# Attention rounds on TensorE in the order scores, values, turns in place of scores, turns, values

## The reference

```python
s = jnp.einsum('bqhd,bkhd->bhqk', q, k) * scale + bias
p = jax.nn.softmax(jnp.where(mask, s, NEG_INF), axis=-1)
o = jnp.einsum('bhqk,bkhd->bqhd', p, v)
```

## Time and profile before

| | |
|---|---|
| median of 3 runs | 1201.32 us (1199.18 to 1202.43) |
| profiled execution | 1197.51 us, span 1195.4 us |
| busy: TensorE, VectorE, ScalarE, GpSimd | 1030.1, 665.0, 476.1, 167.4 us |
| mean granted clock of TensorE | 0.922 of full speed |
| turns L475 | 240 records, median 273 ns |
| values L487 | 160 records, median 275 ns |
| copies L548 | 80, median 471 ns |

### The profile page before, as it was taken

The page is one execution under the profiler, slowest core; times in us unless marked ns, Lnnn a source line. Parts: engine busy times, 40 slices in busy tenths (PEclk is TensorE's granted clock), DMA queues, the critical chain, the costliest instruction groups (busy, mean ns, idle before and its releaser), DMA issues.

```text
span 1195.4 us, 17516 instructions
## 1 busy us (share of the span) xinstructions
PE 1030.1 (86%) x6902; PEld 933.6 (78%) x6902; DVE 665.0 (56%) x1247; ACT 476.1 (40%) x693; POOL 167.4 (14%) x171
## 2 busy tenths in 40 slices
PE   5698967868899779788779999997998878999995
PEld 2597736657899568776769999996996778999994
DVE  5654176867455666463574545456443575454555
ACT  0243333433344553336533443432446443434340
POOL 1001668700096000000001000000001000000000
PEclk9799876979999989888888999998999898999998
DMA  9863424224345503631055545452452053454540
GB/s 371 326 232 110 182 106 159 89 71 141 110 177 192 189 2 134 227 106 36 1 194 194 192 176 195 173 199 86 169 182 86 1 194 133 167 206 162 207 161 35
DMA packets 22535, 181.53 MB, mean 152 GB/s; under 512 B 3599, under 2 KB 3999, under 8 KB 6743
## 3 DMA queue, kind: packets, MB, share of 16 engines
q1 hardware_dynamic: 18112, 167.88, 38.2%
q0 software_dynamic: 2384, 10.88, 2.8%
q10 hardware_dynamic: 1991, 2.12, 0.6%
HBM read 179.82 MB, written 1.05 MB: 151 GB/s over the span
## 4 chain that ended last, share of the span: by engine, by line
PE 71%; DVE 14%; ACT 6%; DMA 4%; issue 2%; POOL 1%; ACTq 1%; SPq 0%; DVEq 0%; POOLq 0%
PE G L777 12%; PE G L778 12%; PE G L779 12%; PE S L842 7%; PE S L844 7%; PE S L843 7%; PE T L396 3%; DMA early<-in_ada_w 3%; DVE wlo L1307 2%; PE T L475 2%; ACT whi L1066 2%; DVE hTl L413 2%; PE S L924 1%; PE G L489 1%; PE G L487 1%
## 5 line engine op out<-in xcount | busy, mean ns | idle before, releaser
L777 PE MATMUL G<-whi,hTh 128*128 128x256 f32 (+4 forms) x884 | 275.3, 311 | 29.3 <-DVE hTl L413 28.1
L778 PE MATMUL G<-wlo,hTh 128*128 128x256 f32 (+4 forms) x884 | 271.3, 307 | 0.0
L779 PE MATMUL G<-whi,hTl 128*128 128x256 f32 (+4 forms) x884 | 270.7, 306 | 0.0
L1307 DVE TENSOR_TENSOR wlo<-ring,whi 128x2048 fp32r<-128x2048 f32 (+4 forms) x56 | 151.3, 2703 | 127.2 <-ACT whi L1066 126.8
L1387 DVE TENSOR_TENSOR wlo<-ring,whi 128x2048 fp32r<-128x2048 f32 x88 | 154.4, 1758 | 110.8 <-ACT whi L1138 83.5
L777 PEld LDWEIGHTS G<-whi,hTh 128*128 128x128 f32 x884 | 175.9, 199 | 37.5 <-DVE hTl L413 33.5
L842 PE MATMUL S<-hTh,whi 128*128 128x256 f32 x704 | 201.0, 285 | 2.8 <-DVE hTl L413 2.8
L843 PE MATMUL S<-hTl,whi 128*128 128x256 f32 x704 | 200.7, 285 | 0.0
L844 PE MATMUL S<-hTh,wlo 128*128 128x256 f32 x704 | 200.7, 285 | 0.0
L778 PEld LDWEIGHTS G<-wlo,hTh 128*128 128x128 f32 x884 | 176.1, 199 | 0.3
L779 PEld LDWEIGHTS G<-whi,hTl 128*128 128x128 f32 x884 | 175.8, 199 | 0.3
(11 more groups left out here) (251 smaller groups left out, 1511.0 us busy)
## 6 DMA issues: line engine op xcount, KB each, us to landing
ring<-in_ffn SPq DMA_DIRECT2D x44, 1536.0 KB, 6.3
ring<-in_ada_w SPq DMA_DIRECT2D x12, 1536.0 KB, 6.4
ring<-in_dil_w_in SPq DMA_DIRECT2D x16, 1024.0 KB, 4.8
ring<-in_cd_w_in SPq DMA_DIRECT2D x10, 1232.0 KB, 5.4
ring<-in_nsa_w_in SPq DMA_DIRECT2D x8, 1432.0 KB, 6.5
early<-in_ada_w SPq DMA_DIRECT2D x4, 1536.0 KB, 25.1
ring<-in_ab_w_in SPq DMA_DIRECT2D x4, 1440.0 KB, 6.2
vec<-in_vecs POOLq DMA_DIRECT2D x11, 512.0 KB, 6.8
```

The costliest lines, as they stand in the source:

```text
L777: pe.matmul(out_, act_h, w_h, start=first_, stop=False)
L778: pe.matmul(out_, act_h, w_l, start=False, stop=False)
L779: return pe.matmul(out_, act_l, w_h, start=False, stop=last_)
L1307: TT(wlo[k % 2][:, 0:cols], raw, whi[k % 2][:, 0:cols].bitcast(F32), ALU.subtract).then_inc(lo_done, 1)
```

## The change

In `att_pe` the block that issues the turns of pair p-1 is moved behind the block that issues the values of pair p-2. Nothing else is changed; waits and semaphores move with their blocks.

```diff
                     if between is not None:
                         between(2 * p)
                         between(2 * p + 1)
-                if 1 <= p < pairs + 1:
-                    for j in (2 * p - 2, 2 * p - 1):
-
-                        pe.wait_ge(att["probs"], 2 * (b0 + j) + 2)
-                        if j >= 2:
-
-                            pe.wait_ge(att["turned"], b0 + j - 1)
-                        for b in range(3):
-                            ins = pe.transpose(TB[j % 2][:, b * P:(b + 1) * P], scr[:, j % 4, 1 + b * P:1 + (b + 1) * P], ident)
-                        ins.then_inc(att["turns"], 1)
                 if p >= 2:
                     back = 1 if out_bank(name, 0) == out_bank(name, 1) else 2
                     if p - 2 >= back:
@@
                         pe.matmul(o[:, 1, :], pt[:, P:2 * P], v[0], start=True, stop=False)
                         pe.matmul(o[:, 1, :], pt[:, 2 * P:SW], v[1], start=False, stop=True).then_inc(att["pv"], 1)
+                if 1 <= p < pairs + 1:
+                    for j in (2 * p - 2, 2 * p - 1):
+
+                        pe.wait_ge(att["probs"], 2 * (b0 + j) + 2)
+                        if j >= 2:
+
+                            pe.wait_ge(att["turned"], b0 + j - 1)
+                        for b in range(3):
+                            ins = pe.transpose(TB[j % 2][:, b * P:(b + 1) * P], scr[:, j % 4, 1 + b * P:1 + (b + 1) * P], ident)
+                        ins.then_inc(att["turns"], 1)
```

## The result

| | before | after |
|---|---|---|
| median of 20 runs each | 1200.12 us (1194.90 to 1203.68) | 1204.29 us (1199.09 to 1209.35) |
| ratio, 95% interval | | 1.0036 [1.0021, 1.0051] |
| profiled execution | 1197.51 us, span 1195.4 | 1204.83 us, span 1202.8 |
| granted clock, mean over the span | 0.922 | 0.913 |

The change costs about 4.2 us. I had predicted 1200.8 us with a range to 1204.0 and a chance of 0.09 for slower: the sign was missed, and the time lies 0.3 us outside the range.

A forecast was written before the change was run, and what follows sets the result against it. TensorE's chain, 71% of the 1195.4 us span, was taken as the bound, with VectorE pacing "nsa". Small terms summed to about -0.3 us, taken as -0.5: 1200.8 us against a median of 1201.32, range 1197.2 to 1204.0.

The forecast's parts named there:

- the rival of the clock: After TensorE's 5.31 us wait in "nsa", full clock comes earlier (about -3 us) or later (+3.5); chance 0.06 each.
- both clock cases: In "nsa", the clock rising earlier, 1198 us, or staying low two rounds more, 1204.3; chance 0.06 each.
- "nsa", start: First pair's values go earlier, VectorE starts about 0.9 us earlier, but a later weight-transfer wait absorbs it: 0.
- "nsa", rounds: Values start unmoved, scores come just in time, low-clock rounds keep the same sum: +0.1 us at most, taken as 0.
- "nsa", end: In the last round with scores, values take the transposes' place and VectorE's 0.35 us wait goes: -0.33 us.
- "dil" and "cd", rounds: TensorE fills the round, so it keeps its 2.96 us; copies still arrive in time: 0.
- "ab", second half: The loop through VectorE and ScalarE shortens by 0.2 us a turn, about two turns: -0.4 us.
- its end: At the end of "ab", the last values must wait for copies of the later transposes: +0.2 us.
- Ends: At the ends of "dil" and "cd", last values wait for copies, partly offset by earlier last scores: +0.1 us each.
- Scores late at any clock: In "nsa", VectorE's next scores 0.3 us late in 13 to 14 rounds: +4, 1204.8 us; chance 0.05.
- gains real and larger: VectorE's results begin earlier in all stages, 0.1 to 0.15 us a round outside "nsa": -3.5, 1197.8 us; chance 0.11.
- the sign of being wrong: Values wait for copies every round, "nsa" scores wait over 0.1 us a round, or stage clock over 0.05 off 0.84.

The follow-up runs named there:

- after_2: The changed kernel, unchanged, traced a second time; single run of 1201.35 us.
- after_3: The changed kernel, unchanged, traced a third time; single run of 1200.04 us.
- nsa_only: The kernel before with the new order in stage "nsa" alone; 1202.30 us, ratio 1.0019 to the kernel before.
- round_12: The kernel before with only round 12 of "nsa" in the changed order; 1201.90 us, ratio 1.0037 to the kernel before.
- new_fill_12: The changed kernel plus one unread 128 x 384 matmul ahead of the values in round 12 of "nsa"; 1200.19 us, ratio 1.0016 to the kernel before.
- new_fill: The changed kernel plus unread 128 x 384 matmuls before the values, 17 in "nsa" and 2 in "dil"; 1198.43 us, ratio 0.9977 to the kernel before.
- new_fill_turns: The changed kernel filled with six unread 128 x 128 transposes in place of each 128 x 384 filler matmul; 1197.72 us, ratio 0.9977 to the kernel before.

## Why the prediction was wrong

**The step that failed** is the claim that the order leaves the clock alone. It was made twice: in the rounds of "nsa" as "the same sum", 0, and against the rival of the clock as "the idle is as long, and the work after it has the same sum". In round 12 of "nsa" neither the length nor the pieces of the idle stayed: 1.75 us in one piece where there were 0.46 and 0.99, in rounds of the same length (5.66 and 5.65 us between the starts of their values). Moving T in this one round makes the clock fall behind it, and one unread matmul in the wait keeps it up. At the low clock the round is no longer VectorE's but TensorE's, and two rounds take 11.5 us instead of 7.9: the term that I had put at 0 measured +3.6 (+3.1 in after_2 and after_3, 11.0 us each).

There is no fixed price per microsecond of low time. Against the kernel before, "nsa" pays 0.23 us for each in the trace of after (3.7 us for 16.3), 0.39 in nsa_only (4.3 for 10.9), 0.15 in round_12 (4.1 for 27.9) and 0.07 in new_fill_12 (0.7 for 9.4). That fits a price that depends on which rounds are low, those of round 12 or others; no run sets a low stretch at will.

I had looked at one wait of 5.31 us only, at the end of which the clock was low already, and had this rival, the clock staying low for two rounds more, at a chance of 0.06 and at that place. There the low stretch got no longer (21 to 35 us of the stage, where it was 21 to 38). Elsewhere two rounds more were low, and its price, +3.5 us and 1204.3 in all, is what was measured. The recorded range was said to take in both clock cases, but it ended at 1204.0, below this price.

**Sizes.** Averages over the traces: "nsa" 91.2 us in the old order without filler (six traces), 95.5 in the changed (five), +4.3; "dil" 31.7 (six with the old order throughout and no filler) and 34.2 (five), +2.5, of which 0.4 is the order itself (31.2 against 30.8 where the low time is 0); "ab" +0.1, "cd" +0.35. That is 7.2 us, more than the 2.5 to 6.1 of the runs' interval. With only the three traces of each kernel, the stages are 5.7 us longer (4.6, 0.7, 0.1 and 0.35), the stretches between them 1.2 us, and "nsa" starts 2.7 us earlier (167.5 against 170.2), in a part where the code is the same and where other kernels' starts lie between 165.7 and 171.4. Together that is the 4.2 us by which the spans differ on average (1200.1 and 1195.9). Why the starts differ I leave open; with three traces it may be chance.

**Point by point.**
- *"nsa", start: 0.* Right, with less won than I said. The result came at 181.63, only 0.3 us earlier (181.92 before, about 181.0 predicted), since V ran at the low clock (its first row takes 0.69 us). L1460 still waits until 188.53, for the same 2.26 us.
- *"nsa", rounds: 0.* Wrong, by the clock. At full clock the scores being "just in time" cost nothing that the traces show: filled, the changed order is no longer than the old.
- *"nsa", end: -0.33.* The wait of 0.35 us is gone at 252.49, as predicted; it is small beside the rest.
- *"dil" and "cd", rounds: 0.* The rounds are 3.00 us (432.57 to 435.57) against 2.96; VectorE's wait has moved, 0.20 ahead of its result and 0.58 ahead of its scores, as predicted.
- *"ab", second half: -0.4, its end: +0.2.* The stage is 0.1 longer. Two of the three waits for copies are shorter (0.34 and 0.33 us), the last is 0.82, and what was saved is not seen in the stage's length; I didn't part it from the end.
- *Ends: +0.1 each in "dil" and "cd".* Under-sized: the stages are +0.4 and +0.35. In "cd", from the V that waits for copies to the last result it is 950.12 to 954.27, 4.15 us, where I had 4.0 and the old order 3.63. So this leg costs 0.52 us, not 0.3 to 0.4, and about 0.2 of it came back in the rest of the stage.
- *Scores late at any clock* (the rival that was to be slower) is rejected by new_fill, where two score steps wait, 1.1 us together, and the stage is no longer for it; *gains real and larger* is rejected by the stages, none of which is shorter on average.

What I had named as the sign of being wrong did show: a clock of "nsa" 0.08 below 0.84, and a score step that waits.

## What to carry to other kernels

Where an engine paces a stage and TensorE waits for it, work of TensorE that stands in the wait is not free to move: before taking a block out of a wait, write down each wait before and after, with its place, and not only the sum, and price the rounds behind it at the low clock too. This names the places to test and is no verdict: here one wait of 1.75 us was followed by the low clock and one of 1.92 was not. If a trace has stretches at half clock right behind waits of one to two microseconds, unread matmuls in those waits are a cheap trial; here they brought 0.2 to 0.3%, with no difference between the orders beyond the intervals. And take several traces of each kernel before reading a clock pattern out of one.

## What the hardware showed that was not expected

- The clock fell to 1.2 GHz behind waits as short as 1.75 and 1.91 us (and of 1.42 us in new_fill), with TensorE busy ahead of them. It did not fall behind the wait of 1.92 us late in "nsa" in the kernel before.
- Once low, it stayed so for about 10 us with TensorE busy without a gap (10.00 of 10.00 us at a clock of 0.54 in the changed kernel), so a busy engine is not enough to tell a full clock from the profile.
- Where it falls differs between executions of one kernel: "dil" had 0 and 3.6 us of low time in three traces of the kernel before, 0 and 6.7 in three of the changed one. The Trainium skill ("TensorE: Matmul & The Clock Gate", Part 1, What's actually happening) says that the chip judges the activity by a window that runs freely and doesn't start with the kernel, so that the moment of a change depends on where the work falls in it. That fits these differences; no run here tests it by itself.
- Transposes as filler kept TensorE's low time as small as matmuls that took the same time did: six transposes (0.92 us in new_fill_turns) in place of one 128 x 384 matmul (0.91 us in new_fill_12) gave 14.4 us of low time in "nsa" with either.
